# Seven half-token block products in place of eight for the gate and up projections of block 2

## The reference

```python
D_MODEL, SEQ, D_FF_2 = 1024, 512, 2816

def swiglu(h, w_gate, w_up, w_down):
    return (jax.nn.silu(h @ w_gate) * (h @ w_up)) @ w_down

x = x + 0.5 * swiglu(rmsnorm(x, ffn1_norm[l]), ffn1_w_gate[l], ffn1_w_up[l], ffn1_w_down[l])
```

## Time and profile before

| | us |
|---|---|
| median of 3 runs | 3445.11 (3443.38 to 3449.31) |
| profiled execution, span from first to last instruction | 3442.4 |
| TensorE matmul busy | 3355.2 (97%) |
| TensorE weight load busy | 2626.8 (76%) |
| VectorE busy | 1669.0 (48%) |
| ScalarE busy | 1222.1 (36%) |
| GpSimd busy | 238.6 (7%) |

### The profile page before, as it was taken

The page is one execution under the profiler, slowest core; times in us unless marked ns, Lnnn a source line. Parts: engine busy times, 40 slices in busy tenths (PEclk is TensorE's granted clock), DMA queues, the critical chain, the costliest instruction groups (busy, mean ns, idle before and its releaser), DMA issues. The chain is left out here.

```text
span 3442.4 us, 42159 instructions
## 1 busy us (share of the span) xinstructions
PE 3355.2 (97%) x15712; PEld 2626.8 (76%) x15716; DVE 1669.0 (48%) x2158; ACT 1222.1 (36%) x1831; POOL 238.6 (7%) x268
## 2 busy tenths in 40 slices
PE   8999999999999999999999999999999999999998
PEld 6667888775688877888775688887888776678887
DVE  6755443666444344443636554435443544654433
ACT  4343122432522233332444443324233344543233
POOL 1200000011000000000103300002000101300000
PEclk9999999999999999999999999999999989999999
DMA  6213322221243232332220133333332321023332
GB/s 169 63 48 86 97 98 97 86 80 49 73 103 95 98 104 73 97 98 98 75 64 25 38 103 97 97 98 94 96 94 97 86 74 32 20 86 98 97 98 67
DMA packets 434263, 288.19 MB, mean 84 GB/s; under 512 B 44529, under 2 KB 412317, under 8 KB 433897
## 3 DMA queue, kind: packets, MB, share of 16 engines
q1 hardware_dynamic: 431272, 280.02, 28.1%
q0 software_dynamic: 2736, 4.58, 0.9%
q10 hardware_dynamic: 144, 2.10, 0.2%
HBM read 284.53 MB, written 2.13 MB: 83 GB/s over the span
## 5 line engine op out<-in xcount | busy, mean ns | idle before, releaser
L2022 PE MATMUL bank<-hh,whi 128*128 128x512 f32 x2768 | 1093.3, 395 | 16.2 <-DVE hl L1470 7.2
L2023 PE MATMUL bank<-hl,whi 128*128 128x512 f32 x2768 | 1080.1, 390 | 0.0
L2024 PE MATMUL bank<-hh,wlo 128*128 128x512 f32 x2768 | 1079.9, 390 | 0.0
L1404 DVE TENSOR_TENSOR wlo<-raw,whi 128x1024 fp32r<-128x1024 f32 (+2 forms) x534 | 646.4, 1212 | 312.4 <-ACT whi L945 298.0
L945 ACT ACTIVATE whi<-raw 128x1024 fp32r<-128x1024 f32 (+2 forms) x534 | 546.4, 1034 | 258.3 <-PE bank L2024 257.9
L2022 PEld LDWEIGHTS bank<-hh,whi 128*128 128x128 f32 x2768 | 521.4, 188 | 150.3 <-issue 33.0
L2024 PEld LDWEIGHTS bank<-hh,wlo 128*128 128x128 f32 x2768 | 521.1, 188 | 109.4
L2023 PEld LDWEIGHTS bank<-hl,whi 128*128 128x128 f32 x2768 | 521.2, 188 | 108.3 <-issue 2.6
L2022 PE MATMUL bank<-fshi,whi 128*128 128x512 f32 (+1 forms) x1358 | 526.3, 388 | 3.6 <-ACT G L1090 1.6
L2023 PE MATMUL bank<-fslo,whi 128*128 128x512 f32 (+1 forms) x1358 | 522.6, 385 | 0.0
L2024 PE MATMUL bank<-fshi,wlo 128*128 128x512 f32 (+1 forms) x1358 | 522.5, 385 | 0.0
(11 more groups left out here) (257 smaller groups left out, 2565.9 us busy)
## 6 DMA issues: line engine op xcount, KB each, us to landing
raw<-in_ffn_w_gate SPq DMA_DIRECT2D x88, 512.0 KB, 3.8
raw<-in_ffn_w_up SPq DMA_DIRECT2D x88, 512.0 KB, 3.8
raw<-in_ffn_w_down SPq DMA_DIRECT2D x88, 512.0 KB, 3.5
raw<-in_w_in SPq DMA_DIRECT2D x78, 512.0 KB, 3.9
raw<-in_w_up SPq DMA_DIRECT2D x64, 512.0 KB, 4.0
raw<-in_w_down SPq DMA_DIRECT2D x64, 512.0 KB, 3.4
raw<-in_w_out SPq DMA_DIRECT2D x16, 512.0 KB, 4.0
raw<-in_w_in SPq DMA_DIRECT2D x18, 256.0 KB, 3.4
```

What stands on the lines that cost most here:

```text
L1404: dve.tensor_tensor(slot3(wlo, s, m), slot3(raw, s, m), slot3(whi, s, m).bitcast(F32), ALU.subtract).then_inc(c.lo_done.sem, 1)
L2022: pe.matmul(o, wh, ah, start=start, stop=False)
L2023: pe.matmul(o, wh, al, start=False, stop=False)
L2024: return pe.matmul(o, wl, ah, start=False, stop=stop)
```

## The change

The first four pairs of each MLP stay as they are. From the fifth on (`PLAIN_T = 4`), a pair is computed as one 2 x 2 block product. The weights' blocks are gate and up by the input features' lower and upper half (each 4 tiles of 128x128, 512 columns of `raw`); the activations' blocks are the lower and upper half of the features by the first and second half of the tokens (256 each). Seven products of combinations of these blocks, each 4 x 3 matmuls of 256 tokens, replace eight; sums of the products give the four corners (gate and up by token half).

- VectorE writes eight tiles x * gain * rstd into `G` (`scaled`) during the second pair, so that the products need no `rstd` afterwards. GpSimd makes four differences of token blocks of 128 x 1024 (`token_sums`). ScalarE and VectorE split the seven moving operands (`moving_high`, `moving_low`); four of them replace `hh` and `hl` in place, which waits for the fourth pair's last matmul, three go to new tensors in free parts of `G` and `tab`.
- For every pair GpSimd makes four combinations of weight blocks, 128 x 512 each (`weight_sums`); the first three wait for the third split of the pair before, the fourth for its sixth. ScalarE and VectorE split seven stationary operands of 128 x 512 (`quad_high`, `quad_low`) into halves of the slots of `whi` and `wlo`, each as soon as the product that used the half is done.
- `lo_done` goes up by two after the seventh split, so both raw slots of a pair come free at once.
- ScalarE copies the fifth product from PSUM (`st_p1`), VectorE adds the products up in five operations (three of 256, two of 512), and multiplies Silu(gate) by up. The last pair's Silu runs inside `down`.
- Products of odd and even pairs use four banks each, so all eight banks are in use.

```diff
+PLAIN_T = 4
+PRODUCTS = 7
+            def weight_sums(c, l, n0, f0, inst):
...
+                    landed(b2, pool, l, n, 0 if i is None else i)
+                    landed(b2, pool, l, n + 1, 0 if i is None else i)
+                    if not first:
+                        pool.wait_ge(c.st_lo.sem, c.st_lo.at(l, q0 + 3))
+                    pool.tensor_tensor(s1, a21, a22, ALU.add).then_inc(c.st_s.sem, 1)
+                    pool.wait_ge(c.st_s.sem, c.st_s.at(l, s0 + 1))
+                    pool.tensor_tensor(s2, s1, a11, ALU.subtract).then_inc(c.st_s.sem, 1)
+                    pool.tensor_tensor(s3, a11, a21, ALU.subtract).then_inc(c.st_s.sem, 1)
...
+                        pool.wait_ge(c.st_lo.sem, c.st_lo.at(l, q0 + 6))
+                    pool.wait_ge(c.st_s.sem, c.st_s.at(l, s0 + 2))
+                    pool.tensor_tensor(s4, a12, s2, ALU.subtract).then_inc(c.st_s.sem, 1)
```

ScalarE, per pair:

```diff
+                    ahead(0)
+                    if i is not None or k:
+                        gate_of(k - 1, i)
+                    for q in (1, 2, 3):
+                        ahead(q)
+                    act.wait_ge(c.st_mm.sem, c.st_mm.at(l, NQ * inst * ST_T + 5 + up_to(NQ, k, i)))
...
+                    act.activation(g(ST_P1, HALF), product_out(k, 4), ACT.Copy).then_inc(c.st_p1.sem, 1)
+                    for q in (4, 5, 6):
+                        ahead(q)
```

VectorE, per pair:

```diff
+                    if later:
+                        first_corner(k - 1, i)
+                    ahead(0)
+                    if later:
+                        gated_product(k - 1, i)
+                    for q in (1, 2, 3):
+                        ahead(q)
...
+                    dve.tensor_tensor(u2, product_out(k, 0), g(ST_P1, HALF), ALU.add).then_inc(c.st_c.sem, 1)
+                    ahead(4)
...
+                    dve.tensor_tensor(u34, pair_of(k, 1), u2.unsqueeze(1).to_broadcast([P, 2, HALF]), ALU.add).then_inc(c.st_c.sem, 1)
+                    ahead(5)
...
+                    dve.tensor_tensor(g(ST_U + HALF, HALF), product_out(k, 2), u34[:, 0, :], ALU.add).then_inc(c.st_c.sem, 1)
...
+                    dve.tensor_tensor(corners, pair_of(k, 3), u34, ALU.add).then_inc(c.u_norm.sem, 1)
+                    ahead(6)
```

TensorE, per pair, and its loop:

```diff
+                    for q in range(PRODUCTS):
...
+                        o, wh, wl = product_out(k, q), half_slot(whi, base, q), half_slot(wlo, base, q)
+                        for n in range(4):
+                            now = slice(P * n, P * n + P)
+                            opens = n == 0 and q in (0, 1, 3, 6)
+                            pe.matmul(o, wh[:, now], moving_hi[q][:, n, :], start=opens, stop=False, skip_group_check=True)
+                            pe.matmul(o, wh[:, now], moving_lo[q][:, n, :], start=False, stop=False, skip_group_check=True)
+                            ins = pe.matmul(o, wl[:, now], moving_hi[q][:, n, :], start=False, stop=n == 3, skip_group_check=True)
...
                 ups(0, 0, 2)
-                with pe.Fori(1, T2 // 2) as i:
-                    ups(i * 4, i * 2)
+                ups(4, 2)
+                products(0)
+                products(1)
+                with pe.Fori(1, ST_T // 2) as i:
+                    products(0, i)
+                    products(1, i)
```

More of the change, by code:

```diff
@@ L41 @@
 X_PARTS = 4
+PLAIN_T = 4
+PRODUCTS = 7
+NQ = PRODUCTS - 1
+HALF = S // 2
 D_IN, FF1, HEADS1 = 3200, 4096, 6
@@ L832, in _, with landed @@
             sp.wait_ge(out_dma, 32 * QT)
+        def landed(b, eng, l, n, more=0):
+            eng.wait_ge(landed_sem[slot_of(b, l, n)], 16 * b["landings"][l][n] + 16 * more)
         @block.gpsimd
@@ new lines, in mlp @@
+                gated(0, first=True)
+                act.preload_act_table_set(SILU_SET)
+                for j in range(4):
+                    if j < 2:
+                        hi(c, b, l, n0 + 6 + j)
+                    else:
+                        for q in ((0, 1, 2, 3), (4, 5))[j - 2]:
+                            quad_high(q, 0)
+                    if j < 3:
+                        moving_high(j)
+                    if j % 2 == 0:
+                        t = j // 2
+                        act.wait_ge(c.g_norm.sem, c.g_norm.at(l, f0 + 2 + t + 1))
+                        act.wait_ge(c.f2_done.sem, c.f2_done.at(l, f0 + 2 + t - 1))
+                        act.activation(rt[t], tmp[t], ACT.Silu).then_inc(c.silu.sem, 1)
@@ new lines, in mlp @@
+                moving_high(3)
+                moving_high(4)
+                quad_high(6, 0)
+                moving_high(5)
+                moving_high(6)
+                product(0)
+                product(1)
+                with act.Fori(1, ST_T // 2 - 1) as i:
+                    act.preload_act_table_set(SILU_SET)
+                    product(0, i)
+                    product(1, i)
+                act.preload_act_table_set(SILU_SET)
+                product(ST_T - 2)
+                product(ST_T - 1)
@@ L1290, in _ @@
+                down(c, b, l, n0 + 2 * T2, f0, T2, c.f2_done, lambda: gate_of(ST_T - 1))
             for l in range(LAYERS):
@@ L1885, in _, with mlp, gated @@
             c, b = c2, b2
-            def mlp(l, n0, f0, d0, r):
-                def gated(i, first=False, last=False):
+            def mlp(l, n0, f0, d0, r, gains):
+                def gated(i, first=False):
                     for j in range(4):
@@ L1908, in gated, with scaled @@
                             dve.tensor_tensor(f, f, rt[t], ALU.mult).then_inc(c.f2_done.sem, 1)
-                gated(0, first=True)
-                with dve.Fori(1, T2 // 2 - 1) as i:
-                    gated(i)
-                gated(T2 // 2 - 1, last=True)
+                inst, base = f0 // T2, slot_of(b, l, n0)
+                def scaled(a, z):
+                    for t in range(a, z):
+                        dve.scalar_tensor_tensor(out=g(XN_AT + S * t), in0=x[:, t, :], scalar=gains[:, t:t + 1], in1=rstd, op0=ALU.mult,
+                                                 op1=ALU.mult).then_inc(c.st_xn.sem, 1)
@@ new lines, in mlp @@
+                gated(0, first=True)
+                lo(c, b, l, n0 + 6)
+                evict_gate(2, 4)
+                moving_low(0)
+                lo(c, b, l, n0 + 7)
+                evict_up(2, 5)
+                moving_low(1)
+                gated_plain(2)
+                for q in range(4):
+                    quad_low(q, 0)
+                evict_gate(3, 6)
+                moving_low(2)
+                for q in (4, 5):
+                    quad_low(q, 0)
+                evict_up(3, 7)
@@ new lines, in mlp @@
+                gated_plain(3)
+                moving_low(3)
+                moving_low(4)
+                quad_low(6, 0)
+                moving_low(5)
+                moving_low(6)
+                product(0)
+                product(1)
+                with dve.Fori(1, ST_T // 2 - 1) as i:
+                    product(0, i)
+                    product(1, i)
+                product(ST_T - 2)
+                product(ST_T - 1)
+                first_corner(ST_T - 1)
+                gated_product(ST_T - 1)
```

193 lines of the change are left out of this document (181 added, 12 removed).

## The result

The changed kernel takes 3426.47 us (median of 4, 3426.04 to 3427.37) against 3444.43 us for the kernel before (median of 4, 3443.38 to 3449.31): ratio 0.9949, 95% interval 0.9935 to 0.9964. It is faster by 18.0 us. The forecast was 50 us (3394), so the sign holds and the size does not: about a third of the gain arrived. The time lies in the stated range of 3370 to 3444, but outside the forecast's own one of 3384 to 3410. It comes nearest to rival A's 3421; that is luck, since A's mechanism, a round of VectorE that is longer than TensorE's, isn't what the traces show.

A forecast was written before the change was run, and what follows sets the result against it. The prediction took TensorE's pace to bound the kernel: 3442.4 - 57.8 (faster matmuls) + 7 (entry and exit) = 3391.6 us, or 3394 as median. Its own range was 3384 to 3410, the stated range 3370 to 3444.

The forecast's parts named there:

- rival A: Steady pairs: VectorE and GpSimd alternate less neatly, their round passes TensorE's at 10.45 us a pair; 3421 us, chance 18%.
- TensorE, 120 ns per 256 columns, 10.08 us a pair: Block-product pairs: 84 matmuls 120 ns apart, weight loads hidden, 0.80 us less per pair, 57.8 us over 72 pairs.
- C: Block-product matmuls: 256 columns pay more for the weight change, 128 ns, 10.75 us a pair; 3443 us, chance 7%.
- D: Block-product matmuls: 113.4 ns each, TensorE 9.52 us a pair, so VectorE's 9.7 sets the pair; 3367 us, chance 8%.
- E: Block-product matmuls: no weight load hides at 256 columns, 19.3 us a pair; 4050 us, chance 1%.
- VectorE's round of 9.7 us hides: Steady pairs: VectorE's work, turns with GpSimd included, takes 9.7 us, under TensorE's 10.08, at 0 cost.
- the 1.2 that the prediction had named as a sign of being wrong: Steady pairs: GpSimd operations with more than 1.2 us of their own would show the forecast wrong; 1.15 was taken.
- B: Steady pairs: every GpSimd operation stops VectorE in full, round 11.7 us, +0.82 a pair; 3511 us, chance 10%.
- Loads at no cost: Steady pairs: both tiles, released together, land in 5.5 us, before their sums start; cost 0.
- Entry and exit of the stage: Each MLP's changed stage: stall about 1.5 us at the fifth pair's fourth product, exit 0.3; together 7 us.
- The exit, 0.3: Stage end: the down products' first tile waits for a split behind one more combination, 0.3 us per MLP.

The follow-up runs named there:

- e9: The e4 kernel with one more GpSimd difference of 128x512 per pair, written to a tile that nothing reads; median 3440.5 us.
- e10: The changed kernel with GpSimd's four differences cut to 128x32 and the first four moving operands taken from plain quadrants (output wrong); median 3396.9 us.
- e5: The changed kernel with 24 bf16 matmuls on other data put into TensorE's gap before the fifth pair's fourth product; median 3425.2 us.
- e7: The changed kernel with copy and split of the first two down tiles ahead of the last pair's combinations; median 3425.8 us.
- e8: The changed kernel with the edits of e4 and e7 together; median 3400.9 us.
- e4: The changed kernel with six plain pairs instead of four ahead of the block products in each MLP; median 3399.4 us.
- e6: The changed kernel with GpSimd's sums for the sixth pair held back until the fourth moving operand is split; median 3425.0 us.
- e1: The changed kernel with the fourth pair's gate evicted and put through Silu ahead of the fifth pair's first four splits; median 3430.0 us.
- e2: The changed kernel with the four token differences made by VectorE in place of GpSimd; median 3417.6 us.

## Why the prediction was wrong, step by step

- **TensorE, 120 ns per 256 columns, 10.08 us a pair:** right (0.12 us apart, 835 matmuls in 100 us). Rivals C, D and E fall. By the rule of the Trainium skill (TensorE: Matmul & The Clock Gate, Part 3, "What overlaps and what doesn't") full-array loads would not hide. The trace disagrees: 84 of them a pair hide, in intervals of 0.12 us.
- **VectorE's round of 9.7 us hides:** right; it is 9.5, the lower bound that the prediction gave. The price of a GpSimd operation was low: 1.15 was taken, and 1.27 to 1.30 us are measured undisturbed, over the 1.2 that the prediction had named as a sign of being wrong. In the steady round that did no harm. e9 shows that the margin was real and thin: one more operation breaks it, as rivals A and B argued for the kernel itself.
- **Loads at no cost:** right; no steady wait of TensorE goes back to them. GpSimd does wait for them, 32.9 us in 100, harmlessly.
- **Entry and exit of the stage, "Stall about 1.5 per MLP; 0 to 6", "Together 4 x 1.8 = 7 us":** this is the step that failed. It measured 10.15 per MLP, 41 in all, with some 9 of the 10.15 at the entry, where 6 was the upper bound. The 34 us of difference are the whole error between 3391.6 and the profiled execution's 3425.3 us of span. The prediction had the right place (the fifth pair's fourth product) and the wrong size, for three reasons. The durations of GpSimd's differences were bounded rightly (2.94 us each, 2.3 to 3.4 forecast), but from a start at 1320.5 where it was 1323.9, with sums by 1341.9, not 1335 to 1339. VectorE's own two-input work beside them was given no extra time: the queue was read as if it ended with the eight scaled tiles, though splits, a product and two operands stand behind them, each waiting a whole GpSimd operation. So nine operations, and not "an eviction and a product", stood ahead of the operand when the fourth pair ended, and "ready some 5 us later" was 10.9 (from 1342.6 to the end of the split at 1353.5). e10 shows that the wait for the fourth pair's last matmul, from which the prediction counted, isn't what makes it late. And the half-clock stretch that follows such a gap had no price (1.5 to 1.9 us a stage, of which e5 got 0.7 back).
- **The exit, 0.3:** 1.0 us of distance, since copy and split stood behind four combinations, not one; e7 and e8 remove it.

The mechanism that the prediction used for the steady round, turns of one whole operation each, is the one that made the entry late; it was applied in one place and left out in the other. In e4 and e10, where VectorE has the time or the work is gone, a stage loses 1.9 us of what its faster matmuls are worth. That this is near the prediction's 1.8 is luck: it had put 1.5 at the fourth product and 0.3 at the exit, and the trace has nothing at the fourth product, some 0.7 behind it and 1.0 at the exit.

Two small slips change nothing: the chain in the earlier trace rows is for the most part, not all, the three matmul lines (24 of PE's 28%), and rival E's 4050 leaves out the 7 us that the other sums hold.

## What to carry to other kernels

Where two engines take turns, write out both queues for the transition into a stage as carefully as for the steady round: the steady round has slack spread over it, while the entry puts one-time work on top of the old stage's work, and its lateness runs through the queue until the first operand that TensorE can't do without. If such an entry stalls, give it more of the old stage to hide behind (two more plain pairs gained some 25 us, though each gives up 0.8 us of saving per MLP) before reordering it. Closing one gap when the engine behind it is late all along only hands the time to the next wait.

## What the runs showed of the hardware

- An idle time of 5.6 us on TensorE was followed in each of the four stages by matmuls at the lower clock (0.21 us apart, granted 0.51 in the window); one of 3.3 us (e6) and the 3.0 us at e9's exit were so too; waits of 0.3 to 0.8 us were not (e4, e10). Matmuls on other data in the gap kept the clock at 1.00 (e5).
- GpSimd's 128x512 operation takes 1.27 to 1.30 us undisturbed (e1, e4), 1.5 to 1.75 in turns with VectorE's splits of 512 and 2.1 to 2.3 with splits of 1024; its 1024-wide difference takes 2.94 in turns, and VectorE makes one in 2.0, itself in turns (e2). VectorE's split of 1024 takes 3.4 beside these, up from 1.23, its longest stretch here.
- 256-column fp32r matmuls, each with a full 128x128 weight load, keep 0.12 us from start to start pair after pair (835 in 100 us), with VectorE and GpSimd at 94 and 65% beside them.
